# SSM heads of a two-block network: chunks of 128 tokens per direction, the mask added on TensorE, and the two directions kept apart until TensorE adds them

## The reference

```
cum = jnp.cumsum(jnp.moveaxis(dt * A, 2, -1), axis=-1)
decay = jnp.exp(jnp.where(tri, cum[..., :, None] - cum[..., None, :], -jnp.inf))
cb = jnp.einsum('bcign,bcjgn->bcgij', Cc, Bc)
y_diag = jnp.einsum('bcghij,bcjghp->bcighp', cb[:, :, :, None] * decay, xdt)
states = jnp.einsum('bcghj,bcjgn,bcjghp->bcghpn', to_end, Bc, xdt)
y_off = jnp.einsum('bcign,bcghpn,bcghi->bcighp', Cc, h_start, jnp.exp(cum))
...
y, _, _ = bidirectional_ssd(xs, dt, A, Bm, Cm, hc_f, hc_b)   # y_f + flip(y_b)
return ssm_output(y, xs, z, D_skip, norm_g, w_out), out_c
```

## Time and profile before

| | |
|---|---|
| median of 3 runs | 1710.42 us (1710.02 to 1713.01) |
| profiled execution | 1713.57 us |
| its span in the trace | 1711.4 us |
| TensorE busy | 1569.1 us (92%) |
| VectorE busy | 792.2 us (46%) |
| ScalarE busy | 622.8 us (36%) |
| mean granted TensorE clock | 0.942 of full speed |

### The profile page before, as it was taken

The page is one execution under the profiler, slowest core; times in us unless marked ns, Lnnn a source line. Parts: engine busy times, 40 slices in busy tenths (PEclk is TensorE's granted clock), DMA queues, the critical chain, the costliest instruction groups (busy, mean ns, idle before and its releaser), DMA issues.

```text
span 1711.4 us, 22672 instructions
## 1 busy us (share of the span) xinstructions
PE 1569.1 (92%) x9342; PEld 1286.0 (75%) x9342; DVE 792.2 (46%) x1389; ACT 622.8 (36%) x1105; POOL 201.0 (12%) x195
## 2 busy tenths in 40 slices
PE   7899999888979897999999998899996889899997
PEld 6878799575835575888888885788984558699997
DVE  6761154333157734223322224866735992154453
ACT  5342244324226625222122215322434760154342
POOL 2000373020000001111011110000000110111011
PEclk9799999897969998999999998999998998899998
DMA  7313645854200023223222322222431222555541
GB/s 238 125 50 123 228 169 192 318 194 171 74 1 0 26 74 147 99 76 110 98 99 83 102 80 101 77 98 99 173 124 50 100 99 74 201 193 167 192 167 43
DMA packets 36109, 206.83 MB, mean 121 GB/s; under 512 B 4952, under 2 KB 9480, under 8 KB 14888
## 3 DMA queue, kind: packets, MB, share of 16 engines
q1 hardware_dynamic: 33344, 200.11, 32.6%
q10 hardware_dynamic: 1848, 2.52, 0.8%
q0 software_dynamic: 816, 2.78, 0.5%
HBM read 202.76 MB, written 2.62 MB: 120 GB/s over the span
## 4 chain that ended last, share of the span: by engine, by line
PE 79%; DVE 9%; ACT 5%; DMA 3%; issue 2%; POOL 1%; SPq 1%; ACTq 0%; DVEq 0%; POOLq 0%
PE lin L1610 17%; PE lin L1612 17%; PE lin L1611 17%; PE lin L1593 7%; PE lin L1716 3%; PE aux L1945 2%; DMA ring<-ada_in 2%; PE modp L1642 2%; PE lin L1968 1%; ACT hn_hi L662 1%; ACT hn L663 1%; PE aux L1658 1%; PE aux L1951 1%; PE aux L2041 1%; DVE arena L1169 1%
## 5 line engine op out<-in xcount | busy, mean ns | idle before, releaser
L576 DVE TENSOR_TENSOR w_split<-ring,w_split 128x1024 fp32r<-128x1024 f32 (+1 forms) x140 | 187.0, 1339 | 383.3 <-ACT w_split L571 383.3
L571 ACT ACTIVATE w_split<-ring 128x1024 fp32r<-128x1024 f32 (+1 forms) x140 | 158.4, 1134 | 478.8 <-PE lin L1612 402.6
L1610 PE MATMUL lin<-hn_hi,w_split 128*128 128x512 f32 (+1 forms) x864 | 304.3, 352 | 14.3 <-DVE hn_lo L863 12.3
L1612 PE MATMUL lin<-hn_hi,w_split 128*128 128x512 f32 (+1 forms) x864 | 300.7, 348 | 0.0
L1611 PE MATMUL lin<-hn_lo,w_split 128*128 128x512 f32 (+1 forms) x800 | 276.3, 345 | 0.0
L1610 PEld LDWEIGHTS lin<-hn_hi,w_split 128*128 128x128 f32 x864 | 164.8, 191 | 42.3 <-DVE hn_lo L863 12.8
L1612 PEld LDWEIGHTS lin<-hn_hi,w_split 128*128 128x128 f32 x864 | 165.4, 191 | 20.6
L1611 PEld LDWEIGHTS lin<-hn_lo,w_split 128*128 128x128 f32 x800 | 153.4, 192 | 16.8
L1610 PE MATMUL lin<-hn_hi,w_split_ssm 128*128 128x512 f32 (+2 forms) x392 | 134.9, 344 | 11.8 <-DVE hn_lo L863 6.1
L1611 PE MATMUL lin<-hid_split,w_split 128*128 128x512 f32 (+1 forms) x416 | 143.2, 344 | 0.0
L1611 PE MATMUL lin<-hn_lo,w_split_ssm 128*128 128x512 f32 (+2 forms) x392 | 133.9, 342 | 0.0
(11 more groups left out here) (360 smaller groups left out, 2594.0 us busy)
## 6 DMA issues: line engine op xcount, KB each, us to landing
ring<-ada_in SPq DMA_DIRECT2D x48, 1024.0 KB, 4.9
ring<-ssm_in_in SPq DMA_DIRECT2D x24, 1024.0 KB, 4.9
ring<-od_in_in SPq DMA_DIRECT2D x12, 1024.0 KB, 4.9
ring<-ffn0a_in_in SPq DMA_DIRECT2D x11, 1024.0 KB, 5.9
ring<-ffn0b_in_in SPq DMA_DIRECT2D x11, 1024.0 KB, 4.8
ring<-ffn1a_in_in SPq DMA_DIRECT2D x11, 1024.0 KB, 4.9
ring<-ffn1b_in_in SPq DMA_DIRECT2D x11, 1024.0 KB, 4.9
ring<-ev_in_in SPq DMA_DIRECT2D x9, 1024.0 KB, 13.4
```

Source lines behind the costliest of these rows:

```text
L571: act.activation(parts[:, 0], w, ACT.Copy).then_inc(sig("w_high"), 1)
L576: dve.tensor_tensor(parts[:, 1], w, parts[:, 0].bitcast(F32), ALU.subtract).then_inc(sig("w_low"), 1)
L1610: mm(lin[0:m, tile % RING, 0:width], hi, x_hi, start=kt == 0, stop=False)
L1612: ins = mm(lin[0:m, tile % RING, 0:width], lo, x_hi, start=False, stop=kt == kts - 1)
```

## The change

Tokens are handled in two chunks of 128 for each direction, as the reference does, in place of 256 at once. The state that enters each chunk is stored apart for each direction (`state_in`). Of the four blocks of a head (2 directions, 2 chunks) each is 128 by 128. The mask is a matmul of an identity with a large constant (bf16), to which TensorE adds the rows; ScalarE takes exponentials straight from PSUM, with the row's own value and log dt as bias; the decay from the start is worked out on 64 rows and spread by TensorE into a `lin` bank. TensorE adds the directions in y's bank. The states between the chunks need B and x of the own tokens in token-major (`bx_tok`), 16 more matmuls (`added_states`) and VectorE's `add_states`.

```diff
-            return aux_of["ssm_heads"] + 5 * g
-
-        def bc_tile(h):
-            return aux_of["ssm_heads"] + 5 * (h // 4) + 1 + h % 4
+            return aux_of["ssm_heads"] + max(5 * g - 2, 0)
+        def rows_tile(h):
+            return aux_of["ssm_heads"] + h + min(1 + (h // 2 + 1) // 2, GROUPS)
+        def since_tile(h):
+            return lin_of["ssm_heads"] + h + max(h // 2 - 2, 0)
+        def y_tile(n):
+            return lin_of["ssm_heads"] + min(2 * n + 6, M_HEADS) + n
...
+                    act.activation(since_rows, rows_g[0:64], ACT.Exp)
+                    act.activation(log_rows, log_rows, ACT.Ln)
+                    act.activation(tot_pick[:, 1:2], tot_pick[:, 0:1], ACT.Exp)
+                    for c, cols in enumerate(chunk_cols):
+                        act.activation(dt_tmp[:, cols], rows_g[0:64, cols], ACT.Exp, scale=-1.0, bias=tot_chunk[:, c:c + 1])
                     act.activation(dt_tmp[:, L:2 * L], dt_tmp[:, L:2 * L], ACT.Exp, scale=-1.0, bias=tot[:, 1:2])\
...
-                between, since = decay[h // 2 % 3][:, h % 2], from_start[h // 2 % 3][:, h % 2]
-                tile = bc_tile(h)
-                act.wait_ge(sig("gaps"), h + 1)
...
-                for d, qt, lo_, hi_, at in (parts[0], parts[3]):
-                    own.mark(act.activation(between[:, at:at + L], aux[:, tile % AUX, d * L:(d + 1) * L], ACT.Relu,
-                                            bias=cols_g[:, 0, qt, d * 32 + h:d * 32 + h + 1]))
-                own.settle()
-                act.activation(between, between, ACT.Exp, scale=-1.0).then_inc(sig("decays"), 1)
-                frees(act.activation(since.rearrange("p a b -> p (a b)"), aux[:, tile % AUX, :], ACT.Exp, scale=-1.0),
-                      "aux", tile)
+                p, e = h // 2, h % 2
+                if h == 0 or h % 4 == 2 and h < M_HEADS - 2:
...
+                    full(act, "aux", cb_tile(g))
+                    frees(act.activation(cb[:, g % 2], aux[:, cb_tile(g) % AUX, 0:L], ACT.Copy), "aux", cb_tile(g))
+                tile = rows_tile(h)
+                full(act, "aux", tile)
...
+                for d in range(2):
+                    for qt in range(QT):
+                        cols = slice((2 * d + qt) * P, (2 * d + qt + 1) * P)
+                        ins = act.activation(decay[p % 3][:, e, cols], aux[:, tile % AUX, cols], ACT.Exp, scale=-1.0,
+                                             bias=cols_g[:, 0, qt, d * 32 + h:d * 32 + h + 1])
+                frees(ins, "aux", tile)
...
+                    for n_ in range(2):
...
+                    for n_, src in enumerate((rows_neg, since_rows)):
+                        own.link(dve.tensor_copy(rows_split[0:64, n_], src))
+                        own.mark(tt(rows_split[64:P, n_], src, rows_split[0:64, n_].bitcast(F32), ALU.subtract))
...
+                    own.mark(tt(rows_neg, rows_neg, log_rows, ALU.add))
+                    own.mark(tt(dt_tmp[:, 0:L], dt_tmp[:, 0:L], dt2[:, 0:L], ALU.mult))
+                    own.mark(ts(since_rows[:, 0:64], ident[0:64, 0:64], tot_pick[:, 1:2], None, ALU.mult))
+                    own.mark(dve.tensor_copy(ident_low, ident[:]))
+                    own.mark(dve.tensor_copy(mask_wide, ssm_mask.unsqueeze(2).to_broadcast([P, 2, QT, P])))
...
+            for q in range(4):
+                if q >= 2:
+                    full(dve, "aux", aux_of[f"states{q - 2}"] + 1)
+                for qt in range(QT):
+                    tile = aux_of[f"xc_tok{q}"] + qt
+                    full(dve, "aux", tile)
+                    for d in range(2):
+                        weights = cols_g[:, 1, qt, d * 32 + 8 * q:d * 32 + 8 * q + 8]
+                        ins = tt(xw[:, q % 2, d, qt, :].rearrange("p (a b) -> p a b", a=8),
+                                 aux[:, tile % AUX].rearrange("p (a b) -> p a b", a=8), each(weights, 64), ALU.mult)
+                    frees(ins, "aux", tile)
...
+                for qt in range(QT):
+                    taken(dve, "aux", aux_of[f"x_tok{q}"] + qt)
+                    weights = cols_g[:, 2, qt, qt * 32 + 8 * q:qt * 32 + 8 * q + 8]
+                    ins = tt(wx[:, q % 2, qt, :].rearrange("p (a b) -> p a b", a=8),
+                             x_tok[:, qt, q * 2 * L:(q + 1) * 2 * L].rearrange("p (a b) -> p a b", a=8),
+                             each(weights, 64), ALU.mult)
+                ins.then_inc(sig("x_weighed"), 1)
...
+                for n in range(2):
+                    g, tile = 2 * q + n, aux_of[f"added{q}"] + n
+                    taken(dve, "aux", aux_of[f"states{q}"] + n)
+                    for d in range(2):
+                        own.mark(tt(state_in[d][1 - d][:, g].rearrange("p (a b) -> p a b", a=4),
+                                    state[:, g, d].rearrange("p (a b) -> p a b", a=4),
+                                    each(total_decay[:, d, 4 * g:4 * g + 4], 64), ALU.mult))
+                    own.settle()
+                    full(dve, "aux", tile)
+                    for d in range(2):
+                        after = state_in[d][1 - d][:, g]
+                        ins = tt(after, after, aux[:, tile % AUX, d * L:(d + 1) * L], ALU.add)
+                    frees(ins, "aux", tile)
...
+            weigh_x(0)
+            weigh_x(1)
+            for q in range(4):
+                add_states(q)
+                if q < 2:
+                    weigh_x(q + 2)
...
-                for h in range(2 * i, 2 * i + 2) if i < DT_ else ():
...
-                    for d, qt, lo_, hi_, at in parts[1:3]:
-                        ins = ts(decay[i % 3][:, h % 2, at:at + hi_ - lo_], aux[:, tile % AUX, d * L + lo_:d * L + hi_],
-                                 cols_g[:, 0, qt, d * 32 + h:d * 32 + h + 1], 0.0, ALU.add, ALU.max)
-                    ins.then_inc(sig("gaps"), 1)
...
+            for p in range(DT_):
+                for h in (2 * p, 2 * p + 1):
+                    tile = since_tile(h)
+                    full(dve, "lin", tile)
+                    frees(tt(from_start[p % 3][:, h % 2], lin[:, tile % RING, :].rearrange("p (a b) -> p a b", a=2),
+                             twice(cm[:, h // 4, :]), ALU.mult), "lin", tile)
                     taken(dve, "aux", cb_tile(h // 4))
-                    dve.wait_ge(sig("decays"), h + 1)
-                    for d, qt, lo_, hi_, at in parts:
-                        m = decay[(i - 1) % 3][:, h % 2, at:at + hi_ - lo_]
-                        ins = stt(out=m, in0=m, scalar=cols_g[:, 1, qt, d * 32 + h:d * 32 + h + 1],
-                                  in1=cb[:, h // 4 % 2, at // L, at % L:at % L + hi_ - lo_], op0=ALU.mult, op1=ALU.mult)
-                    ins.then_inc(sig("mixed"), 1)
-                    taken(dve, "aux", bc_tile(h))
-                    since = from_start[(i - 1) % 3][:, h % 2]
-                    tt(since, since, twice(cm[:, h // 4, :]), ALU.mult).then_inc(sig("c_decayed"), 1)
-                if 3 <= i < DT_ + 2:
-                    y_out(i - 3)
+                    taken(dve, "aux", rows_tile(h))
+                    m = decay[p % 3][:, h % 2].rearrange("p (a b) -> p a b", a=2)
+                    tt(m, m, twice(cb[:, h // 4 % 2]), ALU.mult).then_inc(sig("mixed"), 1)
...
+            turn("bx_tok", lambda n: bm[:, n, 0:L], [(q % 2 * 4, q // 2) for q in range(4)])
+            for q in range(4):
+                turn(f"xc_tok{q}", lambda n: xc[:, n, :], [(4 * q, qt) for qt in range(QT)])
+                if q == 1:
+                    for n in range(AUX):
+                        taken(pe, "aux", aux_of["bx_tok"] + 3 - n)
+                if q:
+                    ssm_states(q - 1)
...
+                pe.wait_ge(sig("x_weighed"), q + 1)
...
+                        ins = mm(aux[:, tile % AUX, qt * L:(qt + 1) * L], bx_tok[:, qt, g * P:(g + 1) * P],
+                                 wx[:, q % 2, qt, n * L:(n + 1) * L], start=True, stop=True)
+                    fills(ins, "aux")
...
+            turn_x(0)
+            ssm_states(3)
+            turn_x(1)
+            for q in range(4):
+                added_states(q)
+                if q < 2:
+                    turn_x(q + 2)
...
-                        for d in range(2):
-                            one = ident_split[0:64, d * 32 + h:d * 32 + h + 1].to_broadcast([64, P])
-                            for part in range(2):
-                                ins = mm(aux[:, tile % AUX, d * L:(d + 1) * L], one, rows_split[0:64, part],
-                                         start=part == 0, stop=part == 1)
...
+                if i == 0 or i % 2 and i < DT_ - 1:
...
+                        ins = mm(aux[:, tile % AUX, cols], bm[:, g, cols], cm[:, g, cols], start=True, stop=True)
+                    fills(ins, "aux")
+                for h in (2 * i, 2 * i + 1) if i < DT_ else ():
+                    pick = [heads_split[:, d * 32 + h:d * 32 + h + 1].to_broadcast([P, P]) for d in range(2)]
+                    tile = rows_tile(h)
```

(19 more changed lines are left out.)

219 lines of the change are left out of this document (95 added, 124 removed), and 3 rows, old and new, of the table AUX_TILES.

## The result

The changed kernel takes 1683.87 us (median of 4 runs, 1679.43 to 1688.21) against 1711.41 us of the kernel before (4 runs), a ratio of 0.9839 with an interval of 0.9802 to 0.9875: 27.5 us faster, where 1683 was forecast. The profiled execution has a span of 1677.9 us.

What follows compares the result with a forecast made beforehand. VectorE's list was taken to bound the heads, TensorE `ssm_in`, and their alternation the states. Heads -29.8, states 0 and `ssm_in` +2.6 sum to -27.2 us, giving 1683 us from the median 1710.42; range 1666 to 1699.

Steps and rivals of the forecast that it cites:

- VectorE's stall goes and TensorE takes over: Heads: VectorE's list falls to 2.8 us a pair and TensorE becomes the bound at 3.8; net -18 to -36, chance 0.62.
- Prices: Heads: paces from the trace give each engine's work per pair: TensorE 3.8 us, VectorE 2.8, ScalarE 2.6 (3.4).
- The 13 pairs: Heads from y(0) to y(13): 13 × 3.8 plus eight ada blocks and two sums, 58.5 us against 76.0 before.
- y is dear: Heads bounded elsewhere or y at 0.084 a record, 2.7 us: +11 us, 1692 to 1704 with states 5 longer; chance 0.18.
- Up to y(0): Start of the heads: TensorE waits for ScalarE's table load and exponentials; y(0) starts at 8.0 us, before 14.9.
- a rival only: Heads: TensorE falls to 1.2 GHz and stays, 1729 us if half clock holds throughout; chance 0.06, partial losses 0.04.
- States: 0, as a gain that is spent: States stage: the double buffer's gain is spent on the new states, 41.7 against 42.1 us; 0, with 5 either side.
- four rounds of 4.4: States stage: TensorE-bound rounds of two states and two transposed tiles, 4.4 us each, 17.7 in all.
- `ssm_in` +2.6: ssm_in: longer lists on dt delay unit 4 by 0.7 us and unit 7 by 1.9; +2.6, from 0.7 to 5.
- the last stretch: End of the heads after y(13): three y's 6.0 and the last sum 1.0, 7.0 us against 12.4 before.

Runs made afterwards that it cites:

- e4_mask_twice: The changed kernel with the matmul that adds the masks issued twice per head: 1693.71 us, ratio 0.9896.
- e7_y_half_cols: The changed kernel with 64 instead of 128 columns in every matmul of y, leaving y out for half of the tokens: 1677.65 us, ratio 0.9789.
- e6_vector_four: The changed kernel with two more unread VectorE products of 512 per head (four a pair): 1704.85 us, ratio 0.9961.
- e8_no_added: The changed kernel without the states handed from chunk to chunk (no weigh_x, added states or add_states): 1673.89 us, ratio 0.9759.
- e2_log_last: The changed kernel with ScalarE's logarithm behind its exponentials at unit 3, one table load less: 1688.96 us in one execution.
- e0_after_again: The changed kernel unaltered, run once more on another run's chip: 1687.72 us, ratio 0.9840.
- e10_gate_at_y: The changed kernel with the two opening ada blocks issued earlier and TensorE's wait for the last added states moved before y(0): 1681.80 us, ratio 0.9823.

## Why the prediction was right, step by step

**VectorE's stall goes and TensorE takes over.** Right, and shown from three sides: TensorE is busy in 56.30 of 56.30 us, all of what `e4_mask_twice` adds to it and `e7_y_half_cols` takes from it shows in the stage, and with 2.4 us a pair more for VectorE (`e6_vector_four`) it becomes the bound again, at 5.36 us a pair.

**Prices.** y was put at 2.0 us (0.0625 a record) and took 1.90 (0.059); masks, rows and start decays of a pair 1.56, measured 1.49; C B 0.48, measured 0.53; an ada block 1.0, a sum 0.55, both right. ScalarE's 8 exponentials of 128 columns run in 2.17 us, 0.387 each, so they start 0.25 apart; 0.26 was forecast. VectorE's list is 2.96 (from `e6_vector_four`), forecast 2.8. The 13 pairs sum to 56.3 instead of 58.5: y and the rows were each priced some 5% too high. The rival "y is dear", 0.084 a record, is excluded by the 0.059.

**Up to y(0).** The step that was off: 8.0 forecast, 10.15 measured. It assumed full clock at the start of the heads, and a wait of TensorE for ScalarE. The row of 3.90 us for a y at half clock was used for a rival only, but VectorE's chain of added states, forecast in the same text, is just such a wait for TensorE. Half clock cost an estimated 2.6 us here: by the paces above, two ada blocks, two C B and the rows of six heads are 7.5 us at full clock, and TensorE is busy in all of the 10.15. So no wait for ScalarE is on the path in this profile. Where the clock stayed up (`e8_no_added`) the stretch took 7.9, of which TensorE's own work is again 7.5. The 8.0 was near to that partly by luck, since it was reached through ScalarE's table load and exponentials. Other profiles with the same code there have 9.0 to 10.3 us, so the miss is not one execution's.

**States: 0, as a gain that is spent.** Right in size (-1.0), and the reason is shown: the buffer alone gives 13.4 us in the kernel before (2.5 of them clock), the added states cost 12.9 in the changed one. The parts came as forecast too: 7.5 us to the first states (7.6), four rounds of 4.4 in 17.7 (17.7), and 16.0 behind them (16.4).

**`ssm_in` +2.6.** The two waits grew by 1.0 (unit 4, forecast 0.7) and 1.56 (unit 7, forecast 1.9), 2.56 in all; the stage is 3.0 longer. The Trainium skill ("ScalarE: Activation LUTs", Table sets: the hidden batching unit) has Ln and Exp in one set, by which unit 7 would not be late. The trace disagrees: the order Exp, Ln, Exp, Silu has four loads of 1.28 us (at 1093.56, 1095.27, 1096.99 and 1099.49), the order Exp, Ln, Silu in `e2_log_last` three, and all but 0.15 us of unit 7's wait goes with the fourth.

**Luck in the total.** The sum was 1.5 us short of the measured -28.7 in the touched stages, and misses cancel in it: the stretch up to y(0) came out 2.1 us longer than forecast and `ssm_in` 0.4, the 13 pairs 2.2 shorter, the states 1.0 and the last stretch 0.8. That the median came within 1 us is partly chance: the four runs lie at 1679.4 to 1688.2.

## What to carry to other kernels

When one engine's list is the bound, price the next engine's list to the same grain before calling the gain: here it was forecast at 3.8 to 5.4 us a pair against 5.85, came out at 3.4 to 5.5, and gave the time of the 13 pairs to within 4%. A wait of the engine that becomes the bound costs more than its length where its clock falls behind it, so put work that depends on nothing into it, as the ada blocks here. Small lists that are moved should go where a unit has the most slack, and apart from each other: with the logarithm last the same two lists cost 0.15 us of waits at units 3 and 4, nothing at 12 and 18, and 7.3 at 26 and 30; with the logarithm in between 1.6 at 3 and 4, and 2.2 at 14 and 16.

## What was not expected of the hardware

- The same code waits differently at unit 4. In all twelve profiles of the changed kernel and its variants unit 4 starts 9.62 to 9.64 us behind unit 3; VectorE sets that. TensorE waits 1.1 to 1.3 us in it where its granted clock over the 8 us from unit 3 on was 0.63 to 0.65, and 2.0 to 2.5 where that was 0.74 to 0.81, since it then was early. Behind the longer wait the clock fell again each time, to between 0.70 and 0.85 over the 4 us that begin 12 us behind unit 3, and unit 7 came 1.6 us later: `ssm_in` took 192.4 instead of 190.8 (`e0_after_again`, `e4_mask_twice`, `e6_vector_four`, `e8_no_added`). A faster TensorE lost time here. Why the clock rose sooner in some executions stays open. The windows from unit 3 on show it, first the changed kernel's first profile, then that of `e0_after_again`:

```profile
1077.01:1085.01 8.00, 8.00 (x23) 6.35 (x24) 7.63 (x19) 2.21 (x3) 0.00 (x0) 0.64 0.38 131
1085.01:1089.01 4.00, 2.75 (x12) 1.98 (x11) 3.90 (x6) 1.24 (x2) 0.00 (x0) 1.00 0.00 0
1089.01:1093.01 4.00, 4.00 (x19) 3.30 (x18) 3.14 (x4) 0.98 (x2) 0.00 (x0) 1.00 0.44 133
```

```profile
1085.38:1093.38 8.00, 7.66 (x24) 5.82 (x24) 7.63 (x19) 2.45 (x4) 0.00 (x0) 0.74 0.40 131
1093.38:1097.38 4.00, 2.37 (x8) 1.95 (x9) 3.90 (x6) 1.01 (x2) 0.00 (x0) 0.87 0.00 0
1097.38:1101.38 4.00, 4.00 (x14) 3.18 (x13) 3.13 (x4) 0.44 (x1) 0.00 (x0) 0.70 0.45 131
```

- The length of a wait alone doesn't tell whether the clock falls. Behind the same wait of 0.89 us among the added states, eight records took 1.97 us in the first profile of the changed kernel (1297.71) and in four others, and 2.8 to 3.5 us in six, such as `e10_gate_at_y`:

```profile
1298.77 3.54 PE L2095 MATMUL aux<-hn,arena 128*128 128x256 f32 x8 [0.89 <-DVE xres L1178]
```

- Unit 3 started between 1077.0 and 1085.9 us in the profiles of kernels that are the same up to there. The runs of one kernel differ by up to 10 us (1683.7 to 1693.4 for the changed kernel) or 13 (1709.4 to 1722.6 for the kernel before). The two profiled executions of the changed kernel differ by 13.7 us, of which 8.4 lie ahead of unit 3, 1.6 in `ssm_in`, 0.6 up to y(0) and 3.2 behind the heads. Why unit 3 starts so differently stays open.
